# GpSimd makes the weight parts of both attentions and the weight rests of the third flow stage

## The reference

```
gate = silu(causal_dwconv3(h @ w_gate));  ffn = (gate * (h @ w_up)) @ w_down
att  = softmax(q @ k.T / 8 + mask (+ forget rows)) @ v          # 16 heads of 64
```

## Time and profile before

| | |
|---|---|
| profiled execution | 4319.69 us, its span 4317.9 us |
| median of the runs | 4320.9 us |
| PE / DVE / ACT / POOL busy | 92% / 49% / 33% / 7% of the span |
| PE clock granted, mean | 0.964 |

### The profile page before, as it was taken

One profiled execution on the slowest core, in us unless ns is written; L12 is line 12 of the kernel. 1 busy time (PEld: TensorE's weight loads), 2 busy tenths in 40 slices (PEclk: granted clock), 3 DMA queues, 4 the chain that ended last, 5 costly groups with the idle time before them and its releaser, 6 DMA issues. The chain is left out here.

```text
span 4317.9 us, 46871 instructions
## 1 busy us (share of the span) xinstructions
PE 3965.7 (92%) x18490; PEld 3230.1 (75%) x18490; DVE 2112.3 (49%) x3258; ACT 1437.9 (33%) x2233; POOL 303.2 (7%) x192
## 2 busy tenths in 40 slices
PE   9998779998899969998989998999998999787998
PEld 7886667887788758776767776777887887666887
DVE  3335563444533355554344646665446564333663
ACT  2222444443322242222332323333323333444332
POOL 0000000000000000003445540000000000000000
PEclk9998999999999989999999999999999999899999
DMA  4332113222233310101222223223332332110332
GB/s 144 98 95 66 32 37 91 80 79 93 83 98 95 96 57 27 31 11 54 66 69 73 81 62 112 84 88 99 97 104 62 94 99 71 58 40 29 103 96 85
DMA packets 94319, 328.05 MB, mean 76 GB/s; under 512 B 10416, under 2 KB 11440, under 8 KB 93744
## 3 DMA queue, kind: packets, MB, share of 16 engines
q1 hardware_dynamic: 94128, 325.40, 24.5%
HBM read 319.06 MB, written 6.29 MB: 75 GB/s over the span
## 5 line engine op out<-in xcount | busy, mean ns | idle before, releaser
L1129 DVE TENSOR_TENSOR s_w_lo<-s_w_raw,s_w_hi 128x1024 fp32r<-128x1024 f32 (+2 forms) x404 | 483.9, 1198 | 664.1 <-ACT s_w_hi L1122 661.2
L1149 PE MATMUL s_acc<-xn_hi,s_w_hi 128*128 128x512 f32 x1824 | 721.4, 396 | 62.3 <-DVE s_w_lo L1129 25.3
L1149 PE MATMUL s_acc<-xn_lo,s_w_hi 128*128 128x512 f32 x1824 | 715.2, 392 | 0.0
L1149 PE MATMUL s_acc<-xn_hi,s_w_lo 128*128 128x512 f32 x1824 | 714.8, 392 | 0.0
L1122 ACT ACTIVATE s_w_hi<-s_w_raw 128x1024 fp32r<-128x1024 f32 (+2 forms) x404 | 415.8, 1030 | 582.6 <-PE s_acc L1149 464.7
L1149 PEld LDWEIGHTS s_acc<-xn_hi,s_w_hi 128*128 128x128 f32 x1824 | 345.9, 190 | 151.1 <-DVE s_w_lo L1129 32.6
L1149 PEld LDWEIGHTS s_acc<-xn_hi,s_w_lo 128*128 128x128 f32 x1824 | 345.6, 189 | 72.8
L1149 PEld LDWEIGHTS s_acc<-xn_lo,s_w_hi 128*128 128x128 f32 x1824 | 345.9, 190 | 72.0 <-issue 1.2
L1149 PE MATMUL s_acc<-hidden_hi,s_w_hi 128*128 128x512 f32 x784 | 305.1, 389 | 0.9 <-DVE s_w_lo L1129 0.9
L1149 PE MATMUL s_acc<-hidden_hi,s_w_lo 128*128 128x512 f32 x784 | 305.0, 389 | 0.0
L1149 PE MATMUL s_acc<-hidden_lo,s_w_hi 128*128 128x512 f32 x784 | 305.0, 389 | 0.0
(11 more groups left out here) (682 smaller groups left out, 7511.2 us busy)
## 6 DMA issues: line engine op xcount, KB each, us to landing
s_w_raw<-in_f_up SPq DMA_DIRECT2D x132, 512.0 KB, 3.8
s_w_raw<-in_g_up SPq DMA_DIRECT2D x64, 512.0 KB, 3.7
s_w_raw<-in_f_down SPq DMA_DIRECT2D x48, 512.0 KB, 3.5
hg_w_raw<-in_hg_w SPq DMA_DIRECT2D x32, 512.0 KB, 4.0
s_w_raw<-in_g_down SPq DMA_DIRECT2D x32, 512.0 KB, 3.7
hg_w_raw<-in_mg_w SPq DMA_DIRECT2D x24, 512.0 KB, 3.8
fox_w_raw<-in_fox_w SPq DMA_DIRECT2D x24, 512.0 KB, 3.6
br_w_raw<-in_mg_w SPq DMA_DIRECT2D x22, 512.0 KB, 3.5
```

Of the source, the lines that this page charges most:

```text
L1129: dve.tensor_tensor(self.lo[:, s % self.SLOTS, 0:cols], self.raw[:, s % self.RAW, 0:cols], self.hi_value[:, s % self.SLOTS, 0:cols], ALU.s ...
L1149: last = pe.matmul(out, w[:, slot, tile_cols(k)], v[:, p.k0 + k, :], start=p.start and k == 0 and n == 0, stop=p.stop and k == p.kt - 1 an ...
```

## The change

```diff
 class Feed:
+    def parts(self, pool, r, m, cols):
+        s, slot = self.at(r, m)
+        pool.wait_ge(self.landed[slot], (r * (self.per // self.slots) + m // self.slots + 1) * 16)
+        if s >= self.slots:
+            pool.wait_ge(self.used, s - self.slots + 1)
+        pool.tensor_copy(self.hi[:, slot, 0:cols], self.raw[:, slot, 0:cols]).then_inc(self.rounded, 1)
+        pool.wait_ge(self.rounded, s + 1)
+        pool.tensor_tensor(self.lo[:, slot, 0:cols], self.raw[:, slot, 0:cols], self.hi_value[:, slot, 0:cols],
+                           ALU.subtract).then_inc(self.parted, 1)
 class Ahead:
-        for m in range(self.slots):
+        for m in range(0 if self.on_pool else self.slots):
             self.feed.load(sp, self.n - 1, m, False, self.w_d[0, :, m, :])
+    def parts(self, pool):
+        for r in range(self.n - 1):
+            for m in range(self.per):
+                self.feed.parts(pool, r, m, D)
...
     def round_next(self, act, r, m):
-        self.feed.round(act, r - 1, m + self.slots, False, D)
+        if not self.on_pool:
+            self.feed.round(act, r - 1, m + self.slots, False, D)
     def vector(self, dve, r, m):
-        self.feed.rest(dve, r - 1, m + self.slots, D)
+        if not self.on_pool:
+            self.feed.rest(dve, r - 1, m + self.slots, D)
...
 def attention(...):
+            @block.gpsimd
+            def _(pool):
+                ahead.parts(pool)
 class Flow:
+    def rests(self, pool):
+        for s in range(len(self.sources)):
+            self.part(pool, s)
     def rest(self, dve, s):
-        if s >= len(self.sources):
-            return
+        if s < len(self.sources) and not self.on_pool:
+            self.part(dve, s)
+    def part(self, eng, s):
         cols = self.sources[s].shape[-1]
-        dve.wait_ge(self.rounded, s + 1)
-        dve.tensor_tensor(...).then_inc(self.parted, 1)
+        eng.wait_ge(self.rounded, s + 1)
+        eng.tensor_tensor(...).then_inc(self.parted, 1)
 def mixer_end(...):
-        f = Flow(c, st)
+        f = Flow(c, st, on_pool=True)
+            @block.gpsimd
+            def _(pool):
+                f.rests(pool)
```

More of the change, by code:

```diff
@@ L300, with __init__ @@
 class Ahead:
-    def __init__(self, st, c, x, w_d, n, inbox, banks, slots, bias=None):
-        self.c, self.x, self.w_d, self.n = c, x, w_d, n
+    def __init__(self, st, c, x, w_d, n, inbox, banks, slots, bias=None, on_pool=False):
+        self.c, self.x, self.w_d, self.n, self.on_pool = c, x, w_d, n, on_pool
         self.inbox, self.banks, self.bias = inbox, banks, bias or {}
@@ L399, in attention @@
         ahead = Ahead(st, c, x, w_d, pairs, [box[:, m, :] for m in range(group + 2)], [pj[:, m, :] for m in range(2)],
-                      3 if group == 1 else 2, bias)
+                      3 if group == 1 else 2, bias, on_pool=True)
         fetch = {3: 0, 6: 1, 7: 2} if group == 1 else {3: 0, 7: 1, 11: 2, 15: 3}
@@ L1092, with __init__ @@
     RAW, SLOTS, BANKS = 2, 3, 6
-    def __init__(self, c, st):
-        self.c, self.st = c, st
+    def __init__(self, c, st, on_pool=False):
+        self.c, self.st, self.on_pool = c, st, on_pool
         self.raw = st.sb("w_raw", [P, self.RAW, D])
@@ L1122, in round @@
         act.activation(self.hi[:, s % self.SLOTS, 0:cols], self.raw[:, s % self.RAW, 0:cols], ACT.Copy).then_inc(self.rounded, 1)
+    def rests(self, pool):
+        for s in range(len(self.sources)):
+            self.part(pool, s)
     def rest(self, dve, s):
-        if s >= len(self.sources):
-            return
+        if s < len(self.sources) and not self.on_pool:
+            self.part(dve, s)
+    def part(self, eng, s):
         cols = self.sources[s].shape[-1]
-        dve.wait_ge(self.rounded, s + 1)
-        dve.tensor_tensor(self.lo[:, s % self.SLOTS, 0:cols], self.raw[:, s % self.RAW, 0:cols],
+        eng.wait_ge(self.rounded, s + 1)
+        eng.tensor_tensor(self.lo[:, s % self.SLOTS, 0:cols], self.raw[:, s % self.RAW, 0:cols],
                           self.hi_value[:, s % self.SLOTS, 0:cols], ALU.subtract).then_inc(self.parted, 1)
```

## The result

The changed kernel takes 4242.5 us (median of 4 runs, 4239.6 to 4257.2), the kernel before 4320.6 beside it: ratio 0.983 [0.980, 0.985]. It is 78 us faster; 63 were forecast (4257), and the time lies inside the range of 4225 to 4300.

The account below looks back on a forecast made before the run. PE, busiest everywhere, was taken to be held up in three stages by DVE waiting for ACT's rounding. From 4320 us, -19, 0, -26 + 3, -17 - 4, -6 and +6 made -63: 4257 us, range 4225 to 4300.

Parts of the forecast that it names:

- `f3u`: Longest part of s3: DVE's tile chain falls below PE's 11.04 us, removing 17 stalls of 1.10 us, -19 us.
- rest of `s3`: Remainder of s3: start +1.5, gating mixer and merge -2, elsewhere GpSimd's time hidden by lead; together about 0.
- `att`, waits and lock: First attention: nine stalls of PE for probabilities go, -26 us; GpSimd's lock over normalise gives back +3.
- `fox`, waits, lock and start: Second attention: waits for probabilities, net of lock and leftover, -17 us; earlier picks at its start -4 us.
- clock: PE's clock in both attentions: less standing brings back some time at the lower level, -6 us, bounds -25 to +3.
- locks not walked: GpSimd holding up DVE on paths the prediction had not traced: +6 us.
- My walk: One ConvGLU tile traced step by step with GpSimd's locks: DVE done at 10.6 us, just below PE's 11.04.
- The causal reading: In both attentions and the ConvGLU, PE's waits arise because DVE stands in its list for ACT's unfinished rounding.
- something late next: Rival, chance 0.15: ACT's move and exponentials become late; half the attentions' and ConvGLU's gain goes, 4290 us.
- No effect: Rival, chance 0.04: the stalls merely move, 4320 us.
- slower: Rival, chance 0.05: the lock serialises GpSimd and DVE at normalise, +95 against -43, ConvGLU +9; 4381 us.
- The lock gives much back: Rival, chance 0.10: 28 pieces each put 1.3 us on a needed normalise, ConvGLU gains only 9 us; 4298 us.

Follow-up runs that it names:

- the split kernel: Changed kernel with VectorE making the rests of the first 18 pieces (merge and following product), GpSimd those from piece 18 on: 4240.3 us.
- `att` alone: Kernel before with only the first attention's weight parts made by GpSimd: 4298.9 us, ratio 0.995.
- the orders: Kernel before, nothing on GpSimd: attentions' rounds and rests moved later, ConvGLU's rest behind the taps, second attention's first picks ahead of first rests: 4228.7 us.
- GpSimd in quarters: Changed kernel with each GpSimd subtraction cut into four over 256 columns and, in the attentions, each rounding into two over 512: 4224.6 us.
- with the copies: Changed kernel with GpSimd copying the raw weights where it subtracted, so the rests are left out of the result: 4208.4 us, ratio 0.974.
- VectorE's half alone: Kernel before with only VectorE's rests in the attentions moved to the end of their units, ScalarE's roundings left in place: 4251.9 us.
- the ConvGLU's order: Kernel before, nothing on GpSimd, with VectorE's rest of the weights in the ConvGLU moved behind its tile's two taps: 4295.2 us.
- `s3` alone: Kernel before with only the rests of s3 on GpSimd: 4306.5 us, ratio 0.997.

## Why the prediction was right, point by point

The sum had five terms. Of the profiles:

| step | forecast | measured |
|---|---|---|
| `f3u` | -19 | -20.4 |
| rest of `s3` | 0 | +8.1 |
| `att`, waits and lock | -23 | -21.4 |
| `fox`, waits, lock and start | -21 | -21.8 |
| clock | -6 | about -15 in `fox`, and a loss within the row of `s3` |
| locks not walked | +6 | in the rows above |
| sum | -63 | -70.3 (medians: -78) |

- **`f3u`: right.** DVE's chain fell under PE's, all 17 waits went, and GpSimd's rest was never late. The tile is 10.88 us and not 11.04: I had added a pitch to a tile whose first matmul comes out of a stall (0.50 us long instead of 0.39). (12.14 - 10.88) x 17 = 21.4, and 20.4 were measured. My walk had DVE's tile at 10.6 us; it is 10.88 less its wait of 0.74, so 10.14, with one long operation in the tiles shown.
- **Rest of `s3`: the step that failed.** "Elsewhere PE has three slots of lead, which hide GpSimd's longer time" holds for the weights. It says nothing of DVE's own operations that GpSimd holds up, and in the merge these are the activations that the next product waits for: +0.6 and +5.0. The start cost 1.2 of the 1.5 forecast. I gave the merge -2, with +3 as the bound; the split kernel, where `s3` falls by 7.7 us, shows that the loss was GpSimd's. Nor did I ask what a new wait of PE does to the clock: of the 5.0 us up to 3.4 are the 6.8 us at the lower level, and only 2.2 are longer waiting for `merged_lo`. 2.0 more in the gating mixer aren't the change's (they are in `att` alone too), and the down projection gave back 1.3.
- **`att`: right in size, and in the units that lose their stalls.** -18.0 by the waits. The lock cost more than the 3 us written for it, at unit 10 (which stood in my list of what would show the theory wrong) and at unit 15 (which did not), 2.0 and 2.5 us from one start of PE to the next in each of two rounds (waits of 1.5 to 1.65 and 2.19 us), 0.2 to 0.5 of which was there before. I placed it near the start of a round; it sits where GpSimd's instruction meets a unit with little cover.
- **`fox`: right for the terms, short by the clock.** Over the whole stage the waits for the probabilities went from 24.3 to 10.4 us, -13.9 (-17 forecast), the start gave -5.9 (-4 forecast: no lock on the picks), and the copies went from 12.8 to 10.8, -2.0. Units 1 and 7 keep gaps of 1.1 and 1.3 us in most rounds. These make -21.8. The stage gained 36.6.
- **The clock: mis-sized, within its bound of -25.** In `fox` the granted clock went from 0.91 of 315 us to 0.96 of 278, that is from 57 to 22 us on the lower of the two levels; where PE works at the lower level it loses half of the time, so up to 17 us. In `att`, where PE's standing fell by as much, the clock did not rise (0.90, 0.89), and in `s3` it fell more often: 51 us at the lower level for 38, a loss of up to 7 us that my term had only as a gain. The other runs bear on `att`. Its clock is 0.91 with the orders, 0.91 with GpSimd in quarters and 0.94 with the copies. Between 60 and 140 us of the stage, the two rounds with the new waits at units 10 and 15, PE is at the lower level for 20.4 us in the changed kernel and for 3.4 to 10.2 in these three, which have shorter waits there or none. So the new waits go with what the clock failed to give back in `att`; no run isolates them.
- **The causal reading: right, and it says more than I drew from it.** I wrote that DVE stands still in its list for a rest whose `hi` ACT hasn't made yet. VectorE's half alone shows that for the attentions, and the ConvGLU's order for `f3u`. If a wait is the cause, the cheaper cure is to move the waiting instruction, and there it gives 66 and 25 us with no lock at all.

The rivals: *something late next* didn't come (the copies' waits fell). *No effect* and *slower* fell. *The lock gives much back* was nearer to the truth than its chance of 0.10 says. My sum had 3 + 2 + 6 = 11 us for the lock; with copies in place of subtractions the kernel is 34 us faster. And without those 11 us my sum was -74, where that kernel measured -112. So the price under the total was 23 us too low and the gain 38 us too low, a good part of both by the clock (in `fox`, 50.6 us shorter than before without long holds, PE is at the lower level for 7 us; it was 58 before and is 21 in the changed kernel). The total came out 15 us short, better than its parts, and that is luck.

On the rule that offloading between GpSimd and DVE "might not help" (the Trainium skill, Perfetto Trace Analysis, Optimizing Scalar/DVE Operations): the runs agree with its reason and not with its outcome: the offload gave -78 us; but the orders alone gave -92. For GpSimd against VectorE operations with two inputs in SBUF or in a two-port mode, the Trainium skill (SBUF — State Buffer, SBUF: two separate sides) has an exclusive lock on the port, held for the whole instruction by whoever starts first. The trace agrees, with 1.01 us beside 1.04 and 2.34 beside 2.35, and operations from PSUM (`pad`, 0.69) untouched.

## What to carry to other kernels

When PE waits for an engine that is half idle, look at what stands ahead of the late operation in that engine's list and what that one waits for; moving it behind, where its own consumer has slack, gave more than giving it to another engine in whole instructions; in `fox`, giving it to GpSimd in short ones gave 8 to 10 us more still. If GpSimd takes work beside a busy VectorE, its price is the length of one of its instructions laid on any VectorE operation that works in SBUF, so cut the instructions short (four quarters for one: 18 us less) and keep them out of stretches where VectorE's short operations feed PE. Count with each new wait of PE what the clock may lose with it: it can be as much as the wait. A sum that comes out right may hold two errors that partly cancel, as here, by luck: a kernel that takes away one suspected cost shows it.

## What the runs showed of the hardware

- GpSimd's hold doesn't depend on how much the VectorE operation does, and a GpSimd instruction with one input holds as one with two does: 128x1 elements took 0.99 us beside a cast and 2.16 beside a subtraction, 0.15 alone.
- It works both ways and alternates: a cast of 1.04 us took 1.52 when VectorE had the port first, a subtraction of 2.34 took 2.80.
- Cutting a subtraction of 128x1024 into four costs 0.76 to 0.78 us each, 30% more in all.
- With a wait of PE of 3.3 us, 2.2 longer than before, the clock fell to the lower level for 6.8 us (2640 to 2647), which cost up to 3.4 us. It did so in the changed kernel and in that with `s3` alone, and in none with VectorE's rests in the merge.
- A stage of unchanged code (`br`) came out at 599 to 600 or at 606 us in different kernels, by one stretch of 10 us at the lower clock, at the same place in all four that have it; the first stage came out at 408 to 412.
